# More expert rows placed in the earlier stages, ten of them ahead of the last group's maxima, and three row loads issued at a stage's end

## The reference, cut to what matters

```python
q = jnp.einsum('btd,dhk->bthk', h, w_query).reshape(B, T, PEER_HEADS, 2, PEER_DKEY // 2)
s = jnp.einsum('bthpk,hpnk->bthpn', q, sub_keys)
sv, si = lax.top_k(s, PEER_TOPK)
...
act = jax.nn.gelu(jnp.einsum('nd,ned->ne', hx, expert_u[ix]))
return jnp.einsum('ne,ned->nd', act * gx, expert_v[ix])
```

## Time and profile before

| | us |
|---|---|
| median of 3 runs | 5694.38 |
| lowest and highest of them | 5690.73, 5697.15 |
| the profiled execution's own time | 5689.15 |
| its span, first to last instruction | 5687.3 |

### The profile page before, as it was taken

The page is one execution under the profiler, slowest core; times in us unless marked ns, Lnnn a source line. Parts: engine busy times, 40 slices in busy tenths (PEclk is TensorE's granted clock), DMA queues, the critical chain, the costliest instruction groups (busy, mean ns, idle before and its releaser), DMA issues. The chain is left out here.

```text
span 5687.3 us, 41931 instructions
## 1 busy us (share of the span) xinstructions
PE 3063.4 (54%) x16118; PEld 2135.7 (38%) x16118; DVE 3900.4 (69%) x4330; ACT 519.7 (9%) x857; POOL 2940.4 (52%) x1532
## 2 busy tenths in 40 slices
PE   5989988989998887999999780000000000000000
PEld 2787954449996865455554440000000000000000
DVE  2330036865544337657775598999999999999998
ACT  1520002412220000000000100000000000000000
POOL 0130013633432202444543108888888888888887
PEclk7999989999999998999999895555555555555555
DMA  9828887950029976979998519999999999999998
GB/s 389 333 96 336 326 314 290 361 206 1 5 90 410 398 290 260 379 292 420 421 420 330 200 52 407 422 417 422 422 421 421 417 422 419 419 409 422 422 421 363
DMA packets 272654, 1886.23 MB, mean 332 GB/s; under 512 B 31748, under 2 KB 36100, under 8 KB 49479
## 3 DMA queue, kind: packets, MB, share of 16 engines
q0 software_dynamic: 194560, 1409.51, 60.4%
q1 hardware_dynamic: 71270, 433.97, 19.5%
q10 hardware_dynamic: 6624, 40.07, 1.7%
HBM read 1867.64 MB, written 15.79 MB: 331 GB/s over the span
## 5 line engine op out<-in xcount | busy, mean ns | idle before, releaser
L215 PE MATMUL ps<-arena_sb 128*128 128x128 f32 (+2 forms) x9216 | 1890.0, 367 | 113.7 <-PEq L1590 32.4
L314 POOL DMA_INDIRECT arena_sb<-peer_v,arena_sb x640 | 1333.7, 2084 | 699.2 <-issue 427.9
L345 DVE CUSTOM_DVE_ANT_0 arena_sb<-arena_sb 128x2048 f32<-128x2048 f32 x640 | 1479.4, 2325 | 210.5 <-DMA arena_sb<-peer_u,arena_sb 210.2
L350 DVE SCALAR_TENSOR_TENSOR arena_sb<-arena_sb 128x2048 f32<-128x2048 f32 x635 | 1493.1, 2351 | 150.5 <-DMA arena_sb<-peer_v,arena_sb 78.4
L215 PEld LDWEIGHTS ps<-arena_sb 128*128 128x128 f32 x9216 | 1327.7, 196 | 693.9 <-issue 308.8
L314 POOL DMA_INDIRECT arena_sb<-peer_u,arena_sb x640 | 1254.3, 1960 | 562.0 <-DVE arena_sb L345 368.1
L261 POOL DMA_DIRECT2D arena_sb<-w_mod x64 | 34.8, 544 | 610.0 <-PE ps L222 483.5
L1459 PE MATMUL ps<-arena_sb 128*128 128x512 f32 x640 | 281.3, 602 | 25.1 <-PEq L1314 24.2
L810 POOL TENSOR_TENSOR arena_sb<-arena_sb 128x1024 f32<-128x1024 f32 x60 | 160.8, 2690 | 247.4 <-ACT arena_sb L1059 184.9
L1378 DVE TENSOR_TENSOR arena_sb<-ps,arena_sb 128x128 f32<-128x128 f32 (+1 forms) x96 | 35.2, 378 | 338.2 <-PE ps L215 326.7
L873 PE MATMUL ps<-arena_sb 128*128 128x64 f32 x1760 | 204.8, 274 | 0.0
(11 more groups left out here) (222 smaller groups left out, 2291.0 us busy)
## 6 DMA issues: line engine op xcount, KB each, us to landing
arena_sb<-w_mod POOLq DMA_DIRECT2D x64, 1024.0 KB, 7.9
arena_sb<-w_qkv SPq DMA_DIRECT2D x48, 1024.0 KB
arena_sb<-w_ga SPq DMA_DIRECT2D x48, 1024.0 KB
arena_sb<-w_gb SPq DMA_DIRECT2D x48, 1024.0 KB
arena_sb<-w_out SPq DMA_DIRECT2D x48, 1024.0 KB
arena_sb<-w_query SPq DMA_DIRECT2D x48, 1024.0 KB
arena_sb<-w_mod SPq DMA_DIRECT2D x32, 1024.0 KB
arena_sb<-w_z SPq DMA_DIRECT2D x24, 1024.0 KB
```

Source lines behind the costliest of these rows:

```text
L215: mm = pe.matmul(out, weights[:, k * P:(k + 1) * P], x[:, k, :], start=(k == 0), stop=(k == chunks - 1))
L314: nc.gpsimd.indirect_dma_start(slot, None, a["peer_v" if adds else "peer_u"], bass.IndirectOffsetOnAxis(ap=g.index[:, p:p + 1], axis=0)).t ...
L345: nc.vector.tensor_tensor_reduce(rows, rows, total, 1.0, 0.0, ALU.mult, ALU.add, g.dots[:, p:p + 1]).then_inc(t.rows_used, 1)
L350: nc.vector.scalar_tensor_tensor(out=total, in0=rows, scalar=g.weight[:, p:p + 1], in1=total, op0=ALU.mult, op1=ALU.add).then_inc(t.rows_u ...
```

## The change

`scores` of the lead group takes four rows and that of the rest group ten, behind "tile" 0, which DVE uses before its first maxima. The latent `qkv` takes 98 rows in place of 85, the rest group's `branches` 76 in place of 72 (28 in place of 24 in its first eight tiles) and its `output_projection` 38 in place of 32. So 423 rows are taken and 857 are left. A new function `gather_ahead` is run by Pool as its last work in the latent groups' `branches`, `merge` and `scores` and in the rest group's `output_projection`: for each of the first three slots it waits until the slot's last row has been used, and issues one of the next three rows into it. `take` of the next stage that uses rows then gives places only to those not issued yet. The three loads at the start of the rest group's `scores` go. `t.user` keeps each slot's last row.

```diff
--- before.py
+++ after.py
@@ -130,7 +130,7 @@
     t.mod_used, t.mod_copied, t.mod_summed, t.mod_row = (t.sem("mod_" + n) for n in (
         "used", "copied", "summed", "row"))
     t.slot_full = [t.sem(f"slot_full{s}") for s in range(6)]
-    t.slot_fills, t.place = [0] * 6, {}
+    t.slot_fills, t.place, t.user = [0] * 6, {}, [-1] * 6
     t.rows_used, t.gelu_done, t.weight_done = (t.sem(n) for n in ("rows_used", "gelu_done", "weight_done"))
     t.rows, t.issued, t.held = 0, 0, 0
 
@@ -289,7 +289,7 @@
         n = min(n, ROWS - t.rows)
         out.append(range(t.rows, t.rows + n))
         t.rows += n
-    for e in range(t.held, t.rows):
+    for e in range(max(t.held, t.issued), t.rows):
         place_row(t, e, (e - t.held) % slots)
     return out
 
@@ -298,6 +298,7 @@
 
     t.slot_fills[s] += 1
     t.place[e] = t.slot[s], t.slot_full[s], 16 * t.slot_fills[s]
+    t.user[s] = e
 
 
 def of_row(t, e):
@@ -325,6 +326,17 @@
         slot, full, _ = t.place[e]
         gather_row(pool, nc, t, a, e, slot, full)
     t.issued = max(t.issued, stop)
+
+
+def gather_ahead(pool, nc, t, a):
+
+
+    for s in range(3):
+        e = t.rows + s
+        after(pool, t.rows_used, t.user[s] + 1)
+        place_row(t, e, s)
+        gather_row(pool, nc, t, a, e, t.slot[s], t.slot_full[s])
+    t.issued = t.rows + 3
 
 
 def weigh(dve, nc, t, e):
@@ -549,7 +561,7 @@
         t.sem("qk_" + n) for n in ("consts_in", "conv_step", "psum_read", "silu_done", "sq_done", "norm_ps", "norm_step",
                                    "qk_done", "gates_ps", "gates"))
     tiles, normed = 3 * H, 2 * H
-    behind = take(t, [0] * tiles if ctx else [0] + [4] * 20 + [3, 2, 0], 6)
+    behind = take(t, [0] * tiles if ctx else [2] + [4, 5] * 10 + [4, 2, 0], 6)
     raw = t.ps[:, 4, 0:32 * nb].rearrange("p (b n) -> p b n", b=nb)
 
     with nc.Block() as block:
@@ -1099,8 +1111,8 @@
         t.sem("br_" + n) for n in ("gm_in", "o_step", "o_root", "oT_ps", "oT_read", "z_read", "o_staged", "vg_bank",
                                    "vg_done", "vg_step", "mix_ps", "mix_read", "u_read"))
     m0 = 3 * H
-    per = 0 if ctx else (1 if nb == 1 else 3)
-    behind = take(t, [per] * H + [per * 9] + [per] * (H - 1) + [0], 4)
+    behind = take(t, [0] * (2 * H + 1) if ctx else [1] * H + [9] + [1] * (H - 1) + [0] if nb == 1 else
+                  [4, 3] * (H // 2) + [27] + [3] * (H - 1) + [0], 4)
     z_behind, vg_behind, u_behind = behind[0:H], behind[H], behind[H + 1:]
 
     with nc.Block() as block:
@@ -1135,6 +1147,7 @@
                     mod_feed(pool, t, a, m)
             else:
                 gather_rows(pool, nc, t, a, behind, 2 * H)
+                gather_ahead(pool, nc, t, a)
 
         @block.tensor
         def _(pe):
@@ -1397,7 +1411,7 @@
     x2_in, gt_in, norm_in, bank_done, part_done, part_added, sq_done, scaled = (t.sem("op_" + n) for n in (
         "x_in", "gt_in", "norm_in", "bank_done", "part_done", "part_added", "sq_done", "scaled"))
     ss = t.stat[:, 0:4 * nb].rearrange("p (b c) -> p b c", c=4)
-    behind = take(t, [3 if last else 0] * (4 * nb - 2) + [2 if last else 0, 0], 4)
+    behind = take(t, [4, 3] * 5 + [3, 0] if last else [0] * (4 * nb), 4)
     if last:
         x_c, gt_c, norm_c = (t.m[:, o:o + D] for o in (C + 6144, C + 8192, HL + 6144))
         total, ss_c = t.group[0].h2[:, 0], t.stat[:, 60:61]
@@ -1506,8 +1520,10 @@
                     pool.wait_ge(part_done, nb * c + b + 1)
                     cols = x[:, b, c * COL:(c + 1) * COL]
                     nc.gpsimd.tensor_tensor(cols, cols, part[:, b], ALU.add).then_inc(part_added, 1)
-                    if not ctx:
+                    if last:
                         gather_rows(pool, nc, t, a, behind, nb * c + b)
+            if last:
+                gather_ahead(pool, nc, t, a)
     t.tiles += KD
 
 
@@ -1586,6 +1602,7 @@
         "keys_in", "query_done", "score_ps", "score_read", "step_done", "exp_done"))
     tiles = 2 * H
     m0 = 6 * H
+    behind = take(t, [0 if ctx else 10 if nb == 3 else 4], 4 if nb == 3 else 3)
 
     with nc.Block() as block:
         @block.sync
@@ -1605,12 +1622,9 @@
                 mod_store(pool, t, M_REST - 1)
                 pool.wait_ge(t.mod_out[0], 128)
                 pool.wait_ge(t.mod_out[1], 128)
-            elif nb == 3:
-                for s in range(3):
-                    e = t.issued
-                    place_row(t, e, s)
-                    gather_row(pool, nc, t, a, e, t.slot[s], t.slot_full[s])
-                    t.issued += 1
+            else:
+                gather_rows(pool, nc, t, a, behind, 0)
+                gather_ahead(pool, nc, t, a)
 
         @block.tensor
         def _(pe):
@@ -1640,6 +1654,7 @@
 
         @block.scalar
         def _(act):
+            gelu_rows(act, nc, t, behind[0])
             for n in range(tiles):
                 if ctx and n % 4 == 0 and n:
                     mod_copy(act, nc, t, (m0 + n) // 4 - 1)
@@ -1721,6 +1736,7 @@
                                                   onehot[u].rearrange("p (b k j) -> p b k j", b=nb, k=TOPK), AX_X, ALU.add)
                 step.step(ins)
 
+            use_rows(dve, nc, t, behind[0])
             for h in range(H):
                 top(2 * h)
                 top(2 * h + 1)
```

## The result

The changed kernel takes 5645.59 us (median of 6 runs, 5640.31 to 5650.04), the kernel before on the same chip 5695.57 (5690.73 to 5697.44): a ratio of 0.9916, 95% interval 0.9906 to 0.9926. That is 50 us faster, where 86 were forecast, and 3.6 us above the upper end of the range. The profiled execution took 5647.58 us, its span is 5645.8. The code that the change doesn't touch, up to the latent `qkv`, took 7.0 us longer in it than in the profile of before (902.0 against 895.0); from there on it is 4743.8 us against 4792.3, 48.5 fewer, which agrees with the medians.

The account below looks back on a forecast made before the run. `experts` was taken as bound by bytes, DMA at 421 GB/s, 2.484 us a row. Terms -91.9 - 3.5 + 5.8 + 0.5 + 3.1 = -86.0 took the median from 5694.4 to 5608 us, range 5592 to 5642.

Parts of the forecast that it names:

- Experts: `experts` stage: 894 rows become 857, 37 rows at 2.484 us each, -91.9 us.
- Latent `qkv`: Latent `qkv`: 13 rows more fit beside the PE's work at cost 0; bound 32 us if DVE sets the pace.
- 5640 by uncovered rows: Rival in the latent `qkv`: DVE becomes the pace, 32 us come back, 5640 us; chance 0.20 for 5620 to 5645.
- 5736 by Pool's queue: Rival in the latent `qkv`: L573 waits behind `gather_rows`, long slot rounds pace tiles, 128 us more, 5736; chance 0.03 for slower.
- Rest `scores`: Rest `scores`: ten rows used near 3229, before the first maxima, cost 0, bound +5 us.
- lead `scores`: Lead `scores`: four rows fit in DVE's wait for the first maxima, cost 0, +2 us as a bound.
- The stage ends: Pool's three issues at rest `output_projection`'s end, +3.1 us (bounds 0, 3.8); elsewhere 1 or 2 each if a row landed late.
- Rest `branches`, z tiles: First eight tiles: four rows more, 2.42 us in each of three tiles, 7.3, less 1.5 in tile 0: +5.8.
- Rest `output_projection`: Rest `output_projection`: six rows more, tail loses the gelu wait and gains one row, +0.5 us (bounds -1.5, +5).
- Lead group: Lead `branches` and `merge`: three loads moved before the boundary shorten the PE's wait for weights, -3.5 us (bounds 0, -7.5).
- `merge`: Rest `merge`: same 144 rows, three there earlier help little, 0 us (bounds -3, +3).

Follow-up runs that it names:

- the run with the late loads: Changed kernel with Pool's three loads ahead in rest `scores` held back until the picks at the stage's end, drain kept: 5655.14 us.

## Why the prediction was wrong

- **Experts** was right: -91.9 forecast, -93.2 measured, and the steady stretch is at 421 GB/s again (160 issues in 400 us). The Trainium skill ("DMA: Bandwidth & Descriptors", Specifications) limits a core to about 358 GB/s; the estimate by it, 108 us for the 37 rows, is not what came.
- **Latent `qkv`** was right: cost 0 forecast, -1.1 measured, with DMA at 352 GB/s. The two rivals that lived there (5640 by uncovered rows, 5736 by Pool's queue) did not happen, although the time came out near the first of them: a time near a rival's says nothing of its cause.
- **Rest `scores`** was right: the first maxima came 29.3 us behind the stage's start (28.3 before), cost +0.9. In lead `scores` +0.5.
- **The stage ends** were the step that failed. The sum had +3.1 for Pool's three issues behind the last L1508 and nothing for the others, "at 1 or 2 us each" if a last row landed late. The idle times at the four ends grew by 6.4, 7.0, 4.9 and 10.0 us, 28.3 together, and 29 us went when Pool no longer waited. The price of a load put ahead of a boundary was taken as its issue (0.95 us); with the drain it is its landing, and without it not even the issue (DVE's idle time at the last boundary was then 2.46 us, less than the 4.30 of before). Three loads are 3.1 MB, 7.5 us at 421 GB/s, and the median from issue to landing was 11.5 us. I knew that all engines meet at a block's end, and did not ask what each must have finished by then. My bounds (0 and 3.8) came from the issue's row alone, and no rival had the landing, so the range had no room for it.
- **Rest `branches`, z tiles.** The mechanism was right (DVE's rows, Pool's issues and the copy are one chain), the size wrong. Forecast was 7.3 for the rows less 1.5 for the first tile. Measured, each apart: the four rows +15.0 (99.6 against 84.6 with three), the rows in place -5.5 (84.6 against 90.1). The mis-sized term is 2.42 for a row; it was 3.75. The lag of the copy behind DVE is no part of it, as it was 2.1 us with three rows too. What I had left out is the clock: the fourth row made the PE's wait 3.15 us, and behind it the clock was at 0.50 for 6.1 us. The traces show its share. With three rows the tiles 2, 4 and 6 take 11.5 to 11.7 us from copy to copy. With four they take 15.8 and 15.6 where the clock had fallen behind the wait before, and 14.6 where it had not. So a row cost some 3.1 us at the full clock and 3.9 to 4.3 with the fall. Why 3.1 and not 2.42 stays open.
- **Rest `output_projection`.** The gelu's wait did leave the tail. In its place DVE waited 2.86 and 2.99 us for the landing of the stage's last rows, and from the PE's end to DVE's last read it is 15.9 us (3201.6 to 3217.5) for 10.8 (3165.2 to 3176.0). I had +0.5 here, with +5 as a bound; it was about 5.
- **Lead group.** Forecast -3.5, in this trace +6.8. What of it is the change stays open. The PE's wait for weights at the start of lead `merge`, which I wanted gone, was 2.45 us for 2.62. The lead pair took 346.8 to 354.6 us in five traces with the loads ahead and the drain, 343.1 to 351.0 in five with the loads and no drain, and 344.1 to 351.3 in four with no loads ahead. That is a mean of 351.0, 347.2 and 347.4, with a scatter as large as the difference. The gain that I forecast shows in none of these means.
- **Scatter of a stage.** Of rest `branches`, +21.8 us, 7 are the boundary and 9.5 the z tiles. The other 5 are partly chance: the run with the late loads has the same code up to there, and 309.6 us where the changed kernel's trace has 318.3.

By the traces the misses, forecast against measured, are 16.0 us in rest `branches`, 10.6 in `output_projection`, 4.8 in `merge`, 10.3 in the lead pair and 1.4 in the two `scores`, less 5.1 in the latent `qkv` and `deltanet`, `expert_input` and `experts`. That makes 38.0, where the sum of -86.0 lies 37.5 from the -48.5 of the traces.

## What to carry to other kernels

Work that is started for the next stage is paid at the boundary by its completion, if anything at the boundary waits for completion; find out what each engine's end of block waits for before you price a prefetch by its issue. The prefetch was good (some 9 to 15 us) and the wait bad (up to 29 us), and only taking them apart showed that; the change as made threw the one away with the other. And where three engines form one chain, an issue that can go ahead of the row loads should stand ahead of them: the copy in front gave 10 us by an edit of the order alone.

## What the runs showed of the hardware

- A block's end with Pool's drain held all engines until the indirect loads had landed: DMA ended in the slice 3229.0 to 3229.5, DVE started at 3231.8; Pool's drain itself lasted from 3217.5 to 3231.5. In the kernel before, leaving out the drain at twelve stage ends gave 0.9988 of the time (0.9979 to 0.9997). Without the drain the boundary came before Pool's second and third issue had begun (3436.2; issues at 3436.90 and 3438.15).
- Pool's `DMA_INDIRECT` took 0.94 to 0.96 us with DVE idle and 2.1 to 3.05 beside DVE's multiply and add of two inputs (rest `branches`: 0.94 to 3.05, median 2.13 over 74). The Trainium skill has the reason as a rule ("GPSIMD Engine Reference", Specifications): Pool shares its SBUF interfaces with VectorE, with contention where a DVE instruction has two SBUF inputs. The trace agrees.
- A PE wait of 3.15 us was followed by a granted clock of 0.50 for 6.1 us, which made the next 32 matmuls 2.6 us longer than at 1.00 (13.13 for 10.49). A wait of 3.23 us in the same stage, until 2282.13, was followed by 1.00: the length of the wait alone doesn't tell.
- Stages with the same code scatter between traces: the lead pair by 8 us (346.8 to 354.6, with the loads ahead and the drain), rest `branches` by 9 (309.6 and 318.3). One trace doesn't settle a few us of a stage.
